# Three decoder layers in one kernel: the dense stages' order, the memory's products dealt out between others, and the small loads sent in order of use

## The reference

```
p = x @ w_in[l]                    # q,k | v | r | a_low (16) | u | v_sgu
y_gla = gla_group(q, k, v, r, a_low, ...)    # gated linear attention, chunks of 64
y_sgu = sgu_group(u, v_sgu, w_s, b_s, ...)   # gelu, norm, 128x128 mixing
x = layer_norm(ALPHA * x + concat(y_gla, y_sgu) @ w_out[l])
q, k, v = x @ wq[l], mem @ wk[l], mem @ wv[l]         # 4 heads of 256, 256 memory rows
x = layer_norm(ALPHA * x + softmax(q k^T / 16) v @ wo[l])
x = layer_norm(ALPHA * x + grouped_moe(x, ...))       # 16 experts, two per token
```

## Time and profile before

| | us |
|---|---|
| median of 3 runs | 1841.75 |
| lowest, highest | 1840.08, 1849.64 |
| the profiled execution | 1847.65 |
| its span | 1845.9 |
| TensorE matmuls busy | 1566.5 |
| VectorE busy | 1311.7 |
| ScalarE busy | 1122.1 |

### The profile page before, as it was taken

How to read it: one execution, slowest core, us unless ns; L and a number is a source line. 1 busy time by engine, 2 the same in 40 slices (tenths; PEclk the granted TensorE clock), 3 DMA queues, 4 the chain that set the end, 5 groups by cost and what they waited for, 6 DMA issues and landing times.

```text
span 1845.9 us, 20944 instructions
## 1 busy us (share of the span) xinstructions
PE 1566.5 (85%) x7971; PEld 1302.9 (71%) x7971; DVE 1311.7 (71%) x1784; ACT 1122.1 (61%) x1335; POOL 32.9 (2%) x67
## 2 busy tenths in 40 slices
PE   3979877999996889985899999488997779999975
PEld 3769755777884768964778777377786557878764
DVE  3567445899997476537699998648555559999963
ACT  3534424889995443432889897256553349899952
POOL 4000000000000100000000000000000000000000
PEclk9989987999998899987999999799988989999988
DMA  8335422999997433623699999243432439999940
GB/s 282 115 126 196 158 91 105 339 369 380 375 383 259 160 129 125 225 67 138 239 380 375 369 382 351 83 154 108 137 127 90 159 108 346 377 369 380 389 191 23
DMA packets 174629, 422.75 MB, mean 229 GB/s; under 512 B 7037, under 2 KB 7201, under 8 KB 174513
## 3 DMA queue, kind: packets, MB, share of 16 engines
q1 hardware_dynamic: 170336, 407.92, 61.5%
q0 software_dynamic: 4176, 13.30, 2.2%
HBM read 420.15 MB, written 1.05 MB: 228 GB/s over the span
## 4 chain that ended last, share of the span: by engine, by line
PE 41%; DVE 32%; ACT 19%; issue 7%; DMA 1%; DVEq 0%; SPq 0%; ACTq 0%
DVE w_low L1476 18%; ACT w_high L1178 13%; PE ps L597 10%; PE ps L598 10%; PE ps L599 10%; DVE out_low L1708 3%; PE ps L791 2%; ACT work L1250 1%; PE ps L674 1%; DMA raw<-in_w_in 1%; PE ps L817 1%; PE ps L778 1%; PE ps L1011 1%; ACT x_odd L1236 1%; PE ps L995 1%
## 5 line engine op out<-in xcount | busy, mean ns | idle before, releaser
L1476 DVE TENSOR_TENSOR w_low<-raw,w_high 128x1024 fp32r<-128x1024 f32 x588 | 694.3, 1222 | 319.0 <-ACT w_high L1178 318.6
L1178 ACT ACTIVATE w_high<-raw 128x1024 fp32r<-128x1024 f32 x588 | 600.4, 1055 | 374.5 <-PE ps L599 352.4
L597 PE MATMUL ps<-w_high,act_high 128*128 128x512 f32 x464 | 192.1, 414 | 41.4 <-DVE act_low L1496 25.9
L598 PE MATMUL ps<-w_low,act_high 128*128 128x512 f32 x464 | 188.6, 406 | 0.0
L599 PE MATMUL ps<-w_high,act_low 128*128 128x512 f32 x464 | 188.0, 405 | 0.0
L817 PE MATMUL ps<-w_high,hT 128*128 128x512 f32 x384 | 156.5, 408 | 0.0
L817 PE MATMUL ps<-w_low,hT 128*128 128x512 f32 x384 | 156.1, 407 | 0.0
L791 PE MATMUL ps<-w_high,x_odd 128*128 128x512 f32 x384 | 152.1, 396 | 0.0
L791 PE MATMUL ps<-w_low,x_odd 128*128 128x512 f32 x384 | 150.1, 391 | 0.0
L597 PEld LDWEIGHTS ps<-w_high,act_high 128*128 128x128 f32 x464 | 92.6, 199 | 66.6 <-issue 47.3
L1476 DVE TENSOR_TENSOR w_low<-work,w_high 128x1024 fp32r<-128x1024 f32 x96 | 113.3, 1224 | 0.0
(11 more groups left out here) (354 smaller groups left out, 2872.9 us busy)
## 6 DMA issues: line engine op xcount, KB each, us to landing
raw<-in_w_up SPq DMA_DIRECT2D x96, 1024.0 KB, 7.5
raw<-in_w_gate SPq DMA_DIRECT2D x51, 1024.0 KB, 7.4
raw<-in_w_down SPq DMA_DIRECT2D x48, 1024.0 KB, 7.4
work<-in_w_gate SPq DMA_DIRECT2D x45, 1024.0 KB, 7.9
x_res<-in_w_down SPq DMA_DIRECT2D x45, 1024.0 KB, 7.2
raw<-in_w_in SPq DMA_DIRECT2D x44, 1024.0 KB, 5.4
raw<-in_w_out SPq DMA_DIRECT2D x12, 1024.0 KB, 4.9
raw<-in_wk_x SPq DMA_DIRECT2D x8, 1024.0 KB, 5.3
```

What stands on the lines that cost most here:

```text
L597: pe.matmul(out, lh, rh, start=first, stop=False)
L598: pe.matmul(out, lh, rl, start=False, stop=False)
L1178: A(split_unit(n)[0], raw_unit(n), ACT.Copy).then_inc(high_ready, 1)
L1476: V.tensor_tensor(split_unit(n)[1], raw_unit(n), split_unit(n)[0].bitcast(F32), ALU.subtract).then_inc(low_ready, 1)
```

## The change

Four things change; the third layer and the expert layers stay as they are.

1. **The start.** x comes in two loads of 128 tokens, each turned as it lands. ScalarE and VectorE convert x first and the six units after it.
2. **Small loads.** POOL makes all constants first, then waits until the first two weight loads have landed, then issues the narrow columns, the rank weights `w_a2` and `b_a` (with a semaphore of their own), the memory, w_s, the norms' parameters and the rest. `colc` is turned after vs, and `rows_raw` lies in another buffer.
3. **Memory.** memT is turned after v instead of before it.
4. **Products dealt out.** k0 goes between r and h, with yT's transposes between its second and third unit. k1 follows h. xv is computed in two halves of 512 columns (`dense_cols` in place of `dense_rows`): xva after k1, with x1T's transposes in its middle, and xvb after q1, with the scores in its middle. The splits' counts and the read-outs on ScalarE and VectorE follow.

```diff
@@ plan
-        for name, c0, small in (("qk", O_Q, ("aT", "z", "memT0", "memT1")), ("v", O_V, ("wsT", "decay", "qT")),
+        for name, c0, small in (("qk", O_Q, ("aT", "z")), ("v", O_V, ("memT0", "memT1", "wsT", "decay", "qT")),
...
+        plan_dense([cols(a["wk_x"][l], 0, j) for j in range(2)], L + "k0a", L + "k0b")
         plan_job(L + "yT0", L + "yT1")
         plan_dense([rows(a["w_out"][l], j) for j in range(4)], L + "h0", L + "h1")
-        for b in range(2):
-            plan_dense([cols(a["wk_x"][l], 512 * b, j) for j in range(2)], L + f"k{b}a", L + f"k{b}b")
+        plan_dense([cols(a["wk_x"][l], 512, j) for j in range(2)], L + "k1a", L + "k1b")
+        plan_dense([cols(a["wv_x"][l], 0, j) for j in range(2)], L + "xva")
         plan_job(L + "x1T0", L + "x1T1")
-        plan_dense([rows(a["wv_x"][l], j) for j in range(4)], L + "xv0", L + "xv1")
         for b in range(2):
             plan_dense([cols(a["wq_x"][l], 512 * b, j) for j in range(2)], L + f"q{b}a", L + f"q{b}b")
+        plan_dense([cols(a["wv_x"][l], 512, j) for j in range(2)], L + "xvb")
@@ sync
-            sp.dma_start(x[:], a["x"][0].rearrange("(t p) n -> p t n", p=P)).then_inc(S["x_loaded"], 16)
+            for t in range(TT):
+                sp.dma_start(x[:, t, :], a["x"][0, t * P:t * P + P, :]).then_inc(x_loaded[t], 16)
@@ gpsimd, behind the constants
+                for i in range(2):
+                    pool.wait_ge(loaded[i], 16)
                 for w, k0, k in ([(a["w_in"][l], O_A, RANK) for l in range(DEPTH)]
...
             def load_layer(l):
+                pool.dma_start(w_a2[0:RANK], a["w_a2"][l]).then_inc(S["rank_loaded"], 16)
+                pool.dma_start(w_a2[RANK:RANK + 1], a["b_a"][l].rearrange("(a n) -> a n", a=1)).then_inc(S["rank_loaded"], 16)
                 pool.dma_start(mem_tok, a["mem"][0].rearrange("(t p) n -> p t n", p=P)).then_inc(S["mem_loaded"], 16)
                 load_mix_params(l)
@@ tensor, dense_cols and dense_turned
+                    if j == 1 and after_two is not None:
+                        after_two()
@@ tensor, the layer
-                turn_tiles(ymix, (L + "yT0", L + "yT1"), S["ymix_ready"], TT * l)
+                operand_ready(L + "memT0", L + "memT1")
+                dense_turned(L + "k0", AUX, lambda: turn_tiles(ymix, (L + "yT0", L + "yT1"), S["ymix_ready"], TT * l))
                 operand_ready(L + "yT0", L + "yT1")
                 dense_rows((L + "h0", L + "h1"), 4)
-
-                operand_ready(L + "memT0", L + "memT1")
-                for b in range(2):
-                    dense_turned(L + f"k{b}", AUX)
-                turn_tiles(x, (L + "x1T0", L + "x1T1"), S["normed"], TT * 3 * l)
-                dense_rows((L + "xv0", L + "xv1"), 4, AUX)
+                dense_turned(L + "k1", AUX)
+                dense_cols(L + "xva", AUX, lambda: turn_tiles(x, (L + "x1T0", L + "x1T1"), S["normed"], TT * 3 * l))
...
+                dense_cols(L + "xvb", AUX, cross_scores)
@@ scalar
-            split(SPLIT)
             for l in range(DEPTH):
                 L = f"{l}."
                 tiles_high(act_high, (L + "xT0", L + "xT1"))
+                if l == 0:
+                    split(SPLIT)
                 split(3)
...
                 read_out(L + "r", silu_r, ACT.Silu)
+                split(2)
                 tiles_high(act_high, (L + "yT0", L + "yT1"))
-                split(8)
+                split(2)
+                act.wait_ge(S["ymix_ready"], TT * (l + 1))
                 for b in range(2):
-                    split(4)
                     for k, ab in enumerate("ab"):
                         f = 4 * b + 2 * k
                         read_out(L + f"k{b}{ab}", kT[:, f:f + 2, :], width=T)
+                    if b == 0:
+                        split(12)
+                split(2)
                 tiles_high(act_high, (L + "x1T0", L + "x1T1"))
-                split(8)
-                for t in range(TT):
-                    read_out(L + f"xv{t}", xv[:, t, :].rearrange("p (b n) -> p b n", b=2))
+                split(2)
+                read_out(L + "xva", xv[:, :, 0:512])
...
+                split(2)
+                read_out(L + "xvb", xv[:, :, 512:1024])
```

More of the change, by code:

```diff
@@ L550, in _ @@
             load_small()
-            chain.link(nc.gpsimd.memset(tri[:], 1.0))
-            for t in range(TT):
[L554 to L559, removed]
-            chain.link(nc.gpsimd.affine_select(later[:], later[:], [[-1, P]], ALU.is_gt, 0.0, base=0, channel_multiplier=1))
-            chain.link(nc.gpsimd.memset(later[LCH:P, 0:LCH], 0.0))
-            chain.link(nc.gpsimd.memset(half[:], 0.0))
-            chain.link(nc.gpsimd.memset(half[0:LCH, 0:1], 1.0))
-            chain.link(nc.gpsimd.memset(half[LCH:P, 1:2], 1.0))
-            chain.link(nc.gpsimd.iota(slot_no[:], [[1, OWN]], base=0, channel_multiplier=0, allow_small_or_imprecise_dtypes=True))
-            nc.gpsimd.memset(st[:], 0.0).then_inc(S["consts_ready"], 1)
             load_norm(0)
@@ L904, in _ @@
                 if l == 0:
-                    begin("colc")
-                    pe.wait_ge(S["rows_loaded"], 48)
-                    rows_n = colc.shape[1]
-                    full(pe.transpose(slot_ps("colc")[:, 0:rows_n], rows_raw, ident[0:rows_n, 0:rows_n]), "colc")
                     pe.wait_ge(S["consts_ready"], 1)
@@ L944, in _ @@
                 dense_cols(L + "vs")
+                if l == 0:
+                    begin("colc")
+                    pe.wait_ge(S["rows_loaded"], 48)
+                    rows_n = colc.shape[1]
+                    full(pe.transpose(slot_ps("colc")[:, 0:rows_n], rows_raw, ident[0:rows_n, 0:rows_n]), "colc")
                 pe.wait_ge(S["kdec_ready"], l + 1)
@@ L1004, in _ @@
                     full(i, L + f"pT{t}")
-                operand_ready(L + "pT0", L + "pT1", L + "xv0", L + "xv1")
+                operand_ready(L + "pT0", L + "pT1", L + "xva", L + "xvb")
                 for k in range(2):
@@ L1753, in _ @@
                     dve.wait_ge(S["consts_ready"], 1)
-                    dve.wait_ge(S["small_loaded"], 96)
-                    wait_full(dve, "colc")
-                    frees(V.tensor_copy(colc[:], slot_ps("colc")[:, 0:colc.shape[1]]), "colc")
-                    wait_released(dve, "colc")
                 wait_full(dve, L + "z")
@@ L1795, in _ @@
                 i.then_inc(S["vnorm_ready"], 1)
+                if l == 0:
+                    dve.wait_ge(S["small_loaded"], 96)
+                    wait_full(dve, "colc")
+                    frees(V.tensor_copy(colc[:], slot_ps("colc")[:, 0:colc.shape[1]]), "colc")
+                    wait_released(dve, "colc")
                 for k in range(PAIRS):
```

76 lines of the change are left out of this document (48 added, 28 removed).

## The result

| | before | after |
|---|---|---|
| median | 1843.15 us (4 runs) | 1800.02 us (4 runs) |
| lowest, highest | 1840.08, 1849.64 | 1796.46, 1804.87 |
| the profiled execution, its span | 1847.65, 1845.9 | 1798.53, 1796.8 |

The ratio is 0.9768 (95% interval 0.9742 to 0.9793), a gain of 43 us; forecast were 37.9.

A forecast was written before the change was run, and what follows sets the result against it. TensorE, busy 85% of the span, was taken as the bound, stopping in dense stages for missing operands. Start, layers and small costs summed to -43.0, clock falls +5.1: 1841.75 - 37.9 = 1804 us, range 1793 to 1818.

The forecast's parts named there:

- narrow product: At the start, the narrow product begins at 29.2 us instead of 45.16, a gain of 16.0.
- new waits: h, q0, second pT: TensorE waits for read-outs that free PSUM slots, three a layer: 2.4, 2.1 to 2.4 and 1.3 us.
- q1's end to xh, besides xv's 10.9: From scores to output product, 21.2 us besides xv's own time; saved 9.5 and 8.1, 8.8 a layer.
- wait for x1 behind two units of xva: Between h and q, k1 and two xva units cover the layer norm by a hair: 0 to 1 us.
- memT's slot, a layer: Behind v, vs waits for the slot of the memory's transposes: +0.8 us a layer, bounds 0 and 3.3.
- u, net of o0, layer 0: In layer 0, u waits for vs's slot, mostly absorbed by the wait at o0: +0.4 us, bounds 0 and 1.5.
- The middle fits best ... I take 26: At the start, the fifth weight load lands at 26 us, between 19.7 at full rate and 31.2 at the contended distance.
- The clock in the new holes: I take half: Six holes in the two layers may each lower TensorE's clock, 1.7 us each: 0 to 10.2, taken as +5.1.
- Rival A: At the start, small loads only move the wait and v starves; only 5 us of gain left: 1815, chance 0.18.
- Rival B: The expert layers, bound by DMA transfers, give the gain back: 1842 us, chance 0.03.
- Rival C: Slot reuse holds up every dense product of a layer; slower from 11 such holes: 1897 us, chance 0.04.
- D: All holes stay at the full clock and the fifth weight load is early: -46.6, 1795 us, chance 0.09.

The follow-up runs named there:

- experiment 2: The changed kernel without POOL's wait for the first two weight loads, so the small loads are issued earlier: 1811.12 us, ratio 0.9828 to the kernel before.
- experiments 2 and 7: For the 7: the changed kernel with POOL's small loads released after the first and fifth weight loads, 1803.94 us; also with read-outs ahead of the last waiting unit, 1794.20.
- experiment 6: The changed kernel with the memory's transposes put back ahead of v: 1798.77 us, ratio 0.9762 to the kernel before.
- experiment 4: The kernel before, unchanged, run once more for a second profile: 1848.82 us, span 1847.0.
- experiment 1: Two kernels, each with part of the change: early x and POOL's wait only, 1821.28 us; dealt-out layers and later memory with the old start, 1821.33 us.
- the start alone: The kernel before with only the early x and POOL's wait, the layers' order and the memory's place as before: 1821.28 us, ratio 0.9894.
- k0 alone: The changed kernel with xv whole again behind x1T and nothing around the scores, k0 still between r and h: 1827.70 us, ratio 0.9923.
- experiment 3: The changed kernel with k0, xva and xvb read out ahead of the last unit that waits for the same product: 1791.93 us, ratio 0.9725.

## Why the prediction was right

1804 was forecast and 1800.0 measured, inside the likeliest case's own range (1795 to 1814). By its steps, in the profiles:

| step | predicted | in the trace |
|---|---|---|
| first wide product | 11.9 | 12.06 |
| narrow product | 29.2 (-16.0) | 27.57 (-17.6) |
| new waits: h, q0, second pT | 2.4, 2.1 to 2.4, 1.3 | 2.38, 2.32, 1.25 |
| q1's end to xh, besides xv's 10.9 | 21.2 | 31.93 - 10.9 = 21.0 |
| wait for x1 behind two units of xva | 0 to 1 | none |
| memT's slot, a layer | +0.8 | 0.25 + 0.47 |
| u, net of o0, layer 0 | +0.4 | 1.55 - (3.50 - 2.37) = +0.4 |
| layer 0, narrow product to xh | | 199.73 to 185.81, -13.9 |
| layer 1, qk to xh | | 209.97 to 199.72, -10.3 |
| two layers, clock as assumed | -27.0 + 5.1 = -21.9 | -24.2 |
| sum | -37.9 | -41.8 |

The mechanism held at each step: the operand's waits went, the waits for slots came where slots were counted, at their sizes. Two terms were mis-sized, both by little.

- "The middle fits best ... I take 26" for the fifth load: it landed at 24.34. The third and fourth landed almost at the full rate (14.45, then before 17.61), since POOL's loads were issued only from 12.33 on; only the fifth was slowed. The Trainium skill ("DMA: Bandwidth & Descriptors", Queues, rings and completion order) has each DMA engine serve its queues in turn. Equal turns would give 5.4 us a load; experiment 2's distances of 6.0 to 6.9 are longer, so turns alone are not the whole of it, and the windows show that the whole rate falls while the narrow loads are under way (experiments 2 and 7). How much each of the two takes isn't shown.
- "The clock in the new holes: I take half", three of six, +5.1: the clock fell behind two of six, q0's in both layers, which is 3.4 us by the same price. The Trainium skill ("TensorE: Matmul & The Clock Gate", What's actually happening) says that the moment of a change isn't tied to the kernel's own time. The traces agree. In the kernel after the fall is behind q0's 2.32 us in both layers and never behind h's 2.38, but in experiment 6, with the same waits, it is behind h's 2.38 us in layer 0 (low at 106 to 112) and behind xh's 2.42 in layer 1 (768 to 774), and behind q0's in neither. So it is no property of q0's wait, and which of the six fell could not have been forecast from their lengths.

Layer 1 gained 3.7 us less than layer 0. Of these, 1.6 lie between h and xh and were forecast (9.5 and 8.1 saved at the scores). The other 2.0 lie between o0 and h, where the clock behind o0 changed sides. By the sum of experiment 4 its fall came to 3.4 us before and 1.7 after in layer 0, where the wait had shrunk from 3.50 to 2.37; in layer 1 it came to 1.7 before and 3.4 after, with the wait at 3.5 both times. The prediction had no term for this.

Rival A (only 5 us of the start left) is out by the narrow product at 27.57, and POOL's wait is a large part of what makes it so: without it the product starts at 34.46, more than half the way to the 40 that A's 5 us would leave. Rival B is out: the expert layers gave nothing back. Rival C (more than 11 slot waits) is out: there are three a layer, as counted. D (warm holes and an early fifth load) was half of what happened: the early load, and four warm holes of six.

What isn't in the sum: the profiles differ by 49.1 us and the changed stretches by 41.8. The other 7.3 lie in code that is the same in both: 3.8 from layer 0's x2T to layer 1's xT, 3.3 behind layer 1's x2T, 0.3 between. Experiment 4 ties both to the clock. Of the 3.8, some 3.1 go with one fall (the two kernels of experiment 1, which lack only that one there, take 321.73 and 321.81), the rest with a shorter one ahead of it. The 3.3 go with a sum of falls that is 5.0 smaller (78.2 and 73.2). The change has no term for them, and they are no gain that another kernel could count on. The medians differ by 43.1, which is 5.2 more than forecast; in the profiles the sum is off by 3.9.

## What to carry to other kernels

Work that covers a wait can be moved only if something else takes the place it leaves: cost the covers of both places as one balance, since here one half alone won 3 us in the stretches it changed, the other 8, and both 24. Where results share slots and an in-order engine frees them, queue a job's read-out ahead of any conversion that waits for the same job's end: 8 us here for a count moved by one at three places of a layer. At the start, hold narrow loads back until the first wide ones are in, and look at which wide load the next consumer needs before tuning further: that load, not the small ones, held up the narrow product in all but the last of these kernels that had the early start. Compare two kernels by the stretches that the edit touches and not by the total alone: unchanged code took up to 6.6 us more or less here, with the clock.

## What the runs showed of the hardware that was not expected

- The same code, from layer 1's x2T to the end, took from 989.65 us (the start alone) to 996.24 (k0 alone) in the profiles of these kernels. The sum of the clock's falls in it went with the time, from 71.6 to 78.3 us.
- A wait of the same length at the same place (2.17 us in the expert layer) was followed by a fall of the clock that came to 3.4 us in both profiles of the kernel before, 1.7 in several of the others and nothing in the kernel after.
- Behind the dense stages' waits of 2.3 to 2.4 us the clock fell at one place in one kernel and at another in the next. With 1 us taken off one of them, the fall stood behind a later wait (experiment 3).
- A few narrow loads halve the stream's rate while they last: 178 and 184 GB/s instead of 388 with six loads of narrow columns and the two of the rank weights under way (experiment 7), with the DMA engines shown as busy throughout. The 1 MB of the memory did not do that.
